# Two-layer hybrid block on one core: the input loaded ahead of the constants and turned pair by pair, and the last unit of the output product computed in two passes

## The reference

```
def reference(x, ...):
    x = first_block(x, ...)      # h = x + hybrid(rmsnorm(x, norm_w)); rmsnorm(h)
    return second_block(x, ...)  # below
...
def first_block(...):            # its first step
    u = _rmsnorm(h, norm_w)                  # (256, 2048)
    proj = jnp.matmul(u, w_in)               # mLSTM, delta net, gates: 22576 columns
    ...
def second_block(...):           # its last steps
    mixed = jnp.concatenate([oa, ob], axis=-1) @ w_out[layer]
    h = h + gate[:, None] * mixed
    return rmsnorm(h, final_g)               # (256, 2048)
```

## Time and profile before

| | |
|---|---|
| Median of the runs | 2005.97 us |
| The profiled execution, own time | 2010.53 us |
| Its span in the trace | 2008.5 us |
| TensorE busy with matmuls | 1942.3 us (97%), 11910 instructions |
| VectorE, ScalarE, GpSimd busy | 1372.4 (68%), 960.1 (48%), 263.2 us (13%) |
| GpSimd's 96 issues of `w_mod` loads (L1298) | 69.4 us busy, 0.72 each |
| Mean DMA rate over the span | 195 GB/s |
| Chain that ended last: TensorE, VectorE, GpSimd, ScalarE, DMA | 82%, 6%, 4%, 4%, 1% |

### The profile page before, as it was taken

How to read it: one execution, slowest core, us unless ns; L and a number is a source line. 1 busy time by engine, 2 the same in 40 slices (tenths; PEclk the granted TensorE clock), 3 DMA queues, 4 the chain that set the end, 5 groups by cost and what they waited for, 6 DMA issues and landing times.

```text
span 2008.5 us, 29314 instructions
## 1 busy us (share of the span) xinstructions
PE 1942.3 (97%) x11910; PEld 1711.6 (85%) x11910; DVE 1372.4 (68%) x1895; ACT 960.1 (48%) x1396; POOL 263.2 (13%) x433
## 2 busy tenths in 40 slices
PE   5999989999999999999999899999999999999997
PEld 5988989877888898988888788989898998988885
DVE  4676666665888888798867648656455566656674
ACT  5565655563633333444444355554433355554543
POOL 1027061623111111111110100100000000011000
PEclk9999999999999999999999999999999999999999
DMA  6555453544688887777787866765556534344553
GB/s 210 151 158 153 126 156 116 165 137 144 219 287 273 266 262 255 228 251 236 263 282 249 274 220 198 231 193 189 185 172 198 156 127 162 122 160 154 179 179 125
DMA packets 184663, 392.21 MB, mean 195 GB/s; under 512 B 12569, under 2 KB 12849, under 8 KB 183377
## 3 DMA queue, kind: packets, MB, share of 16 engines
q1 hardware_dynamic: 166240, 321.95, 49.4%
q0 software_dynamic: 17424, 66.72, 11.1%
q10 hardware_dynamic: 864, 1.67, 0.2%
HBM read 386.08 MB, written 4.22 MB: 194 GB/s over the span
## 4 chain that ended last, share of the span: by engine, by line
PE 82%; DVE 6%; POOL 4%; ACT 4%; issue 3%; DMA 1%; SPq 0%; ACTq 0%; DVEq 0%; POOLq 0%
PE GB L2004 48%; PE GB L2008 24%; POOL TB L1021 2%; POOL XB L1024 2%; DVE WL L1952 2%; PE SB L381 1%; ACT WH L1948 1%; PE SB L1634 1%; PE SB L1346 1%; PE SB L1110 1%; PE SB L1735 1%; PE SB L1626 1%; PE SB L1742 1%; DMA wm<-in_w_mod 1%; DMA xin<-in_x 1%
## 5 line engine op out<-in xcount | busy, mean ns | idle before, releaser
L1952 DVE TENSOR_TENSOR WL<-raw,WH 128x1024 fp32r<-128x1024 f32 x608 | 734.6, 1231 | 263.4 <-ACT WH L1948 261.4
L1948 ACT ACTIVATE WH<-raw 128x1024 fp32r<-128x1024 f32 x608 | 625.4, 1057 | 371.3 <-PE GB L2004 247.2
L2004 PE MATMUL GB<-WH,uH 128*128 128x512 f32 x896 | 283.5, 398 | 0.0
L2004 PE MATMUL GB<-WH,uL 128*128 128x512 f32 x896 | 278.7, 392 | 0.0
L2004 PE MATMUL GB<-WL,uH 128*128 128x512 f32 x896 | 277.6, 391 | 0.0
L2008 PE MATMUL GB<-uH,WH 128*128 128x256 f32 x1280 | 215.1, 291 | 5.2 <-DVE WL L1952 5.2
L1328 DVE SCALAR_TENSOR_TENSOR macc<-wm,csil,macc 128x512 f32<-128x512 f32 x300 | 209.4, 748 | 9.5 <-DMA wm<-in_w_mod 8.3
L2008 PE MATMUL GB<-uL,WH 128*128 128x256 f32 x1280 | 207.2, 285 | 0.0
L2008 PE MATMUL GB<-uH,WL 128*128 128x256 f32 x1280 | 206.9, 284 | 0.0
L2004 PEld LDWEIGHTS GB<-WL,uH 128*128 128x128 f32 x896 | 169.5, 189 | 36.2
L2004 PEld LDWEIGHTS GB<-WH,uL 128*128 128x128 f32 x896 | 169.4, 189 | 36.2
(11 more groups left out here) (394 smaller groups left out, 2220.9 us busy)
## 6 DMA issues: line engine op xcount, KB each, us to landing
raw<-in_w_in SPq DMA_DIRECT2D x512, 512.0 KB, 4.6
wm<-in_w_mod POOLq DMA_DIRECT2D x96, 512.0 KB, 5.8
raw<-in_w_out SPq DMA_DIRECT2D x96, 512.0 KB, 5.3
xin<-in_x SPq DMA_DIRECT2D x4, 512.0 KB, 6.7
E<-decay_rows POOLq DMA_DIRECT2D x4, 512.0 KB, 5.4
hres<-in_x POOLq DMA_DIRECT2D x1, 2048.0 KB, 10.8
cin<-in_ctx POOLq DMA_DIRECT2D x1, 2048.0 KB, 8.5
h_spill<-hres POOLq DMA_DIRECT2D x2, 1024.0 KB, 5.5
```

Of the source, the lines that this page charges most:

```text
L1948: e.activation(WH[s % NH][:, :, :], raw[s % NR][:, :, :], ACT.Copy).then_inc(*wh.inc("WH", s))
L1952: e.tensor_tensor(WL[s % NH][:, :, :], raw[s % NR][:, :, :], f32(WH[s % NH][:, :, :]), sub).then_inc(*wl.inc("WL", s))
L2004: m = e.matmul(banks[j][:, :], x[:, c, 128 * j:128 * j + 128], w[:, k, :], start=first, stop=last, skip_group_check=True)
```

## The change

**Start.** `vcol` moves from ScalarE's queue to SyncE's, behind the four loads of `xin` and ahead of the weights. `wsm` and `rb` move to GpSimd's queue, where they and the seven tables of constants are issued once the raw tile of slot 2 has landed. GpSimd clears `wsL` with its other clears, and the squares' scratch gets memory of its own (`p9` 31 to 52). `newton_dve` has four steps in place of five. `xin` is scaled in pieces of 512, 512 and 1024 columns per half ("a", "b", "c"); pairs 0 and 1 wait for piece a, pairs 2 and 3 for b, the others for c. Two pairs are turned before slot 0, and one after each of the slots 0 to 5. Slot 0's split stands ahead of the scaling on ScalarE and behind a and b on VectorE; piece c is scaled later. TensorE starts with `busy_pe`: 59 matmuls of 128 by 128 ones into a bank that is not read, 24 at once, 12 after the third quarter of `xin` has landed, 14 after the fourth, 9 after the squares' sum.

**End.** The last unit ("out", 3) has its eight slots computed for token half 0 alone (48 matmuls), and behind the last slot for half 1 alone (48 more). All eight slots' weights must therefore stay: `place(s)` puts three of them in new buffers `WX0` to `WX2`, and the last three in those of the slots eight before; `split_until` lets the splits run up to two slots further ahead there. Half 0 has its sum, root, scaling and store (`last_dve`, `last_act`) while the second pass runs. Half 1 is finished after it in two pieces of 256 columns, with its own root; VectorE scales columns 0 to 639 and 640 to 1279, ScalarE 1280 to 2047, and SyncE stores all. Squares go to `hfin` in place of `hres`.

```
-    steps("u", -1, 3, 100)
-    steps("u", 0, 5)
+    steps("u", -1, 2, 100)
+    steps("u", 0, 6)
...
-                    [pad("p9", 31), ("s_junk", [128, D], F32)],
+                    [pad("p9", 52), ("s_junk", [128, D], F32)],
...
+        XPARTS = {"a": slice(0, 512), "b": slice(512, 1024), "c": slice(1024, 2048)}
+        def scaled_act(e, c):
+            e.activation(xin[:, 1, XPARTS[c]], xin[:, 1, XPARTS[c]], ACT.Copy, scale=st[:, 5:6]).then_inc(*nx_act.inc("x1" + c))
+        def scaled_dve(e, c):
+            e.tensor_scalar(xin[:, 0, XPARTS[c]], xin[:, 0, XPARTS[c]], st[:, 4:5], None, mul).then_inc(*nx_dve.inc("x0" + c))
+        def busy_pe(e):
+            for said, n in ((init.at("ones"), 24), ((x_in[2], 16), 12), ((x_in[3], 16), 14), (nx_dve.at("ss"), 9)):
+                e.wait_ge(*said)
+                for _ in range(n):
+                    e.matmul(SB[3][:, 0:128], ones[:, :], ones[:, :], start=True, stop=True, skip_group_check=True)
...
+        def place(s):
+            if s < NS - 6:
+                return WH[s % NH], WL[s % NH]
+            if s < NS - 3:
+                return WX[s - (NS - 6)][:, 0], WX[s - (NS - 6)][:, 1]
+            return WH[(s - 8) % NH], WL[(s - 8) % NH]
         def split_act(e, s):
-            if s >= NH:
-                e.wait_ge(*slot.at("mm", s - NH))
+            if NS - 6 <= s < NS - 3:
+                e.wait_ge(*tr_pe.at("t", TOB + 3))
+            elif s >= NH:
+                e.wait_ge(*slot.at("mm", s - (NH if s < NS - 6 else 8)))
...
+        def split_until(s):
+            return 1 if s < 0 else min(NS, s + min(AHEAD, s + 1) + 1 + min(2, max(0, s - (NS - 11))))
...
+            if unit.mode == "tok":
+                m = tokens_pe(e, unit, s, banks, (0,) if last_unit else (0, 1))
...
+            if s == NS - 1:
+                for i in range(8):
+                    m = tokens_pe(e, unit, NS - 8 + i, banks, (1,))
+                m.then_inc(*last_pe.inc("mm"))
...
         @block.gpsimd
+            e.memset(f32(wsL[:, :, :]), 0.0).then_inc(*zero.inc("L"))
+            e.wait_ge(raw_in[2], 16)
+            e.dma_start(wsm[:, :, :], A["c_wsm"]).then_inc(wsm_in, 16)
+            e.dma_start(rb[:, :], A["c_rb"]).then_inc(rb_in, 16)
...
-            e.wait_ge(*nx_act.at("s3"))
-            e.memset(f32(wsL[:, :, :]), 0.0).then_inc(*zero.inc("L"))
```

More of the change, by code:

```diff
@@ L1905, in out_dve @@
             e.wait_ge(*slot.at("mm", end("out", n)))
[L1906 to L1911, removed]
-        def out_scale_dve(e, n):
-            s = slice(512 * n, 512 * n + 512)
-            for i in range(2):
-                e.wait_ge(*of_act.at(f"q{i}", n))
-                e.tensor_tensor(res[:, i, s], res[:, i, s], fg[:, s], mul).then_inc(*fm_dve.inc(f"m{i}", n))
@@ L1997, in product_pe, with tokens_pe @@
             e.wait_ge(*wl.at("WL", s))
+            if unit.mode == "tok":
+                m = tokens_pe(e, unit, s, banks, (0,) if last_unit else (0, 1))
+            else:
+                m = channels_pe(e, unit, s, banks)
+            m.then_inc(*slot.inc("mm", s))
+            if s == NS - 1:
+                for i in range(8):
+                    m = tokens_pe(e, unit, NS - 8 + i, banks, (1,))
+                m.then_inc(*last_pe.inc("mm"))
+        def tokens_pe(e, unit, s, banks, halves):
+            i, (wh_, wl_) = SLOTS[s][1], place(s)
@@ L1998, in product_pe @@
             for k in range(2):
                 H, L, c = moving(unit, 2 * i + k)
-                for n, (x, w) in enumerate(((H, WH[h]), (L, WH[h]), (H, WL[h]))):
-                    first, last = i == 0 and k == 0 and n == 0, i == 7 and k == 1 and n == 2
-                    if unit.mode == "tok":
-                        for j in range(2):
-                            m = e.matmul(banks[j][:, :], x[:, c, 128 * j:128 * j + 128], w[:, k, :], start=first, stop=last,
-                                         skip_group_check=True)
-                    else:
-                        for j in range(4):
-                            m = e.matmul(half(banks[j // 2], j % 2), w[:, k, 128 * j:128 * j + 128], x[:, c, :],
-                                         start=first and j % 2 == 0, stop=last, skip_group_check=True)
@@ L2010, in product_pe, with channels_pe @@
-            m.then_inc(*slot.inc("mm", s))
+                for n, (x, w) in enumerate(((H, wh_), (L, wh_), (H, wl_))):
+                    for j in halves:
+                        m = e.matmul(banks[j][:, :], x[:, c, 128 * j:128 * j + 128], w[:, k, :],
+                                     start=i == 0 and k == 0 and n == 0, stop=i == 7 and k == 1 and n == 2,
+                                     skip_group_check=True)
+            return m
+        def channels_pe(e, unit, s, banks):
+            i, (wh_, wl_) = SLOTS[s][1], place(s)
+            for k in range(2):
+                H, L, c = moving(unit, 2 * i + k)
+                for n, (x, w) in enumerate(((H, wh_), (L, wh_), (H, wl_))):
+                    for j in range(4):
+                        m = e.matmul(half(banks[j // 2], j % 2), w[:, k, 128 * j:128 * j + 128], x[:, c, :],
+                                     start=i == 0 and k == 0 and n == 0 and j % 2 == 0, stop=i == 7 and k == 1 and n == 2,
+                                     skip_group_check=True)
+            return m
```

187 lines of the change are left out of this document (115 added, 72 removed).

## The result

The changed kernel takes 1993.63 us (median of 4 runs, 1993.49 to 1995.29) where before takes 2006.83 beside it (4 runs, 2004.99 to 2008.3): a ratio of 0.9935, 95% interval 0.992 to 0.995. The forecast was 1988.1 with a range of 1985.0 to 1993.5. It was right that the change makes the kernel faster and wrong in the size, by 5.5 us. The profiled execution took 1993.67 us itself, its span is 1991.6.

The account below looks back on a forecast made before the run. TensorE, busy 97% of the span, bounds the kernel, so only its start and end can win. Profiled span 2008.5 - 12.8 - 5.1 = 1990.6 us; carried to the median of 2005.97, the forecast was 1988.1, range 1985 to 1993.5.

Parts of the forecast that it names:

- The price of `busy_pe`'s matmuls: At the start, ones matmuls taken as 0.22 us each slow, four 0.44 fast; all done by about 11.1 us.
- Rival 1's second case: Clock never rises before slot 0; the last 9 ones matmuls hold up pair 0 by 2.6 us more: 1993.0 (rival 1: 25%).
- X: Landing of the last quarter of `xin` at the start: 8.7 us, gain 4.4, bounds 8.0 and 9.6.
- The chain from X to slot 0: Squares, mean, root, scaling, transposes and turning at the start: slot 0 at X + 5.95 = 14.65 us, in place of 25.54.
- Slots 0 to 5: First six slots with a pair turned after each, 6 x (2.88 + 0.44) us; slot 6 at 34.6, before 47.4.
- rival 1: Clock not held in the 3.4 us before slot 0; 2.3 us given back, 1990.4; chance 25%.
- My line of 1.9 us: TensorE idle time after which a row shows a clock fall; neither gap before slot 0 reaches it, so slot 0 fast.
- Rivals 2 to 4: `xin` not earlier, 1992.5 (8%); one-bank passes at the end not overlapping, 2003.6 (2%); slower through late `wsm`, 2010 (2%).
- Rival 5: At the start, GpSimd's DMA issues hold VectorE, piece c ends 0.7 us later: 1988.3; chance 10%, within the forecast's range.
- The end: After the last matmul: span ends 8.8 us later in place of 13.9, gain 5.1 us, bounds 4.1 and 5.6.
- T: The end of the last matmul, from which the kernel's closing steps are counted.
- the sum of 17.9: Whole forecast gain in us: 12.8 at the start and 5.1 at the end, nothing in the middle.

Follow-up runs that it names:

- few: The changed kernel with 44 matmuls of ones (24, 12 and 8) in place of 59; median 1992.4 us, ratio 0.9916 to before.
- after_again: The changed kernel itself, timed and profiled a second time beside other kernels; 12.2 us under before, slot 6 at 40.1 us.
- Few_whole: Against few, the third piece's scaling moves ahead of slot 0 and all pairs wait for `c`; slot 6 at 37.88 us.
- few_const: Against few, `vcol`, `rb` and `wsm` back on ScalarE's queue and the tables issued at once; slot 6 at 41.8 us, 5.7 us later.

## Why the prediction was wrong

- **The price of `busy_pe`'s matmuls failed.** "Four of 128 columns take 0.44 fast, so 0.22 slow each" was read off transposes. A matmul of two plain float32 operands is two records and 0.23 us fast, 0.44 slow. The 35 matmuls behind the third quarter's landing are then 8.1 us and end at 16.6, not at 11.1. Pair 0 waited 3.1 us; few measured it as 3.14. Had the term been priced at 0.23, the forecast's own sum would have shown that TensorE, not the input, was late. Nor was the rise of the clock a fixed one, as the sum took it after the first 24: with a later rise after_again paid 0.8 us more. Rival 1's second case had the right place, the ones holding up pair 0, but by 2.6 us and only under a clock that never rises; that its 1993.0 lies near the measured time is chance.
- **X was 9.82, not 8.7**: 1.1 us, beyond the bound of 9.6. The weak stretch of the earlier trace rows did come back in part, 246 GB/s from 6.0 to 7.0 us; it was given as a bound and left out of the value. By the windows up to there it is worth some 0.5 us, an estimate: the forecast's 2.17 MB have moved by 8.5 us instead of 8.0. The rest is that `xin` does not go alone: until 9.8 us the windows add up to 2.70 MB, so other transfers, most likely those issued behind it, had moved 0.5 MB before its last quarter landed. Eleven other profiles with the input's transfers first have 9.2 to 10.1. What slows the transfers near 6.5 us was not found; it stands in every trace at the same place.
- **The chain from X to slot 0 was right.** The inverse root was forecast for X + 2.65 and came at X + 2.6; both engines scaled beside the split. Without the ones slot 0 would start at X + 6.1 (19.03 - 3.1 - 9.82), forecast X + 5.95. The mean's instruction lost its stall: 0.17 us, where all four profiles with GpSimd's clear in its old place have 1.66.
- **Slots 0 to 5** with their transposes: 20.26 us instead of 19.9. Slot 0's 3.13 and one slot of 3.03 are the rest. No slot waited.
- **The clock** was held (rival 1 did not happen in the changed kernel). My line of 1.9 us without a matmul is not a fixed one: a wait of 2.14 us had a fall behind it in one trace and none in another. Few_whole stood still for about 1.8 us ahead of its transposes, few_const for 2.70, and only the second was slow afterwards.
- **Rivals 2 to 4** did not happen: few_const shows that the order of the transfers is what brings `xin` forward (11.94 with the constants beside it, 9.65 in few); the one-bank passes ran at 27.67 / 122 = 0.227 a matmul; `wsm`, issued at 14.60, landed 5.9 us later and was first read at 42.0. Rival 5 was not put to the test: GpSimd's nine issues stand from 14.60 to 19.51, and VectorE's piece c only starts at 19.67 (0.75 us, as priced). What VectorE did under them, `uL` of pairs 0 and 1 at 18.10, took 0.83 us a pair, and 0.84 before.
- **The end was right**: 9.0 us behind T, forecast 8.8, no wait in the passes, 4.9 for 5.1.
- **From the profile to the median**: the sum of 17.9 was set against one execution and carried over to the median. That was sound for start and end (12.2 to 13.2 timed, 13.0 in the trace). It took the middle for unchanged, since everything follows TensorE's slots; there the two profiled executions differ by 3.9 us, the wait for `lamt` and one fall of the clock. That they do so because everything stands 8 us earlier is likely, but not shown.

Of the 5.5 us between forecast and measurement 3.1 are the ones, 1.1 is X, 0.5 is the rest of the start, 0.2 the end; 0.6 is left, less than one fall of the clock. This is by the first profile.

## What to carry to other kernels

Work that is put in to keep an engine busy has a price from the moment the real work is ready: size it by its measured duration in the slowest form that it can take, count the trace's records against the instructions in the code, and gate it so that it ends before the real input. A wait behind one large transfer on a shared queue, in the middle of the kernel, was worth about as much here (some 7 us for four smaller transfers) as the whole new start. When a change moves time by hardly more than the spread of executions, take out what makes the spread in both kernels and compare those, but look at the spread again: here it went from 5.3 to 1.0 us in one kernel and stayed at 3.6 in the other.

## What the hardware did that was not expected

- A float32 matmul of 128 columns: two records, 0.23 us at the full clock. In the type fp32r, on the same tile, one record, and 0.22 us at the lower clock, which it did not leave in 7.7 us back to back.
- The same 24 matmuls of ones from 1.06 us on raised the clock by 5.0 us in one execution of the changed kernel and only by 7.5 in the next, and slot 6 moved by 0.8 us with it.
- The clock fell behind one wait of 2.14 us and not behind another of the same length.
- In every profile the moved bytes are low from 6.0 us on (140 GB/s from 6.5 to 7.0 in before, 246 in after), until 8 us with the constants in flight and until 7 without.
- The granted clock stands at 1.00 in the windows of slot 0 of before, though its matmuls ran at half speed: at the start only the durations show the level.
